# Attention scores of a hybrid decoder layer: native fp32 on 64-row tiles of TensorE in place of a two-term split

## What is computed

```python
# q: 1024 x 8 heads x 64;  k, v: 1024 x 2 kv heads x 64;  4 query heads share one kv head
scores = einsum('bnqhgd,bnkhd->bnhgqk', qb, kk) * 64 ** -0.5   # per block of 128 queries: 256 keys
scores = where((diff >= 0) & (diff < 128) & (kpos >= 0), scores, -1e30)
probs  = softmax(concat([scores, sink]))[..., :256]
out    = einsum('bnhgqk,bnkhd->bnqhgd', probs, vv)
```

## Time and profile before

| | us |
|---|---|
| median of 3 runs | 949.88 |
| lowest, highest | 949.42, 950.1 |
| the profiled execution | 949.13 |
| its span, first to last instruction | 947.3 |
| TensorE (PE) busy in it | 938.1 |
| VectorE (DVE) busy | 657.3 |
| ScalarE (ACT) busy | 435.9 |

### The profile page before, as it was taken

One profiled execution on the slowest core, in us unless ns is written; L12 is line 12 of the kernel. 1 busy time (PEld: TensorE's weight loads), 2 busy tenths in 40 slices (PEclk: granted clock), 3 DMA queues, 4 the chain that ended last, 5 costly groups with the idle time before them and its releaser, 6 DMA issues.

```text
span 947.3 us, 11501 instructions
## 1 busy us (share of the span) xinstructions
PE 938.1 (99%) x4423; PEld 778.5 (82%) x4423; DVE 657.3 (69%) x713; ACT 435.9 (46%) x651; POOL 189.3 (20%) x182
## 2 busy tenths in 40 slices
PE   8999999999999999999999999999999999999997
PEld 7988888888888888888888888888888888888886
DVE  6645797666655899777777787778776653535668
ACT  5525445544433555445444544344444454435353
POOL 3301000000111424242223243443431100000021
PEclk9999999999999999999999999999999999999999
DMA  6999971005322236386343446464647776677545
GB/s 225 271 343 213 210 145 46 23 23 178 134 89 90 89 107 205 133 190 177 123 133 100 145 118 131 107 143 111 138 90 208 212 235 210 220 267 259 186 154 200
DMA packets 114248, 151.16 MB, mean 160 GB/s; under 512 B 6289, under 2 KB 66193, under 8 KB 114193
## 3 DMA queue, kind: packets, MB, share of 16 engines
q1 hardware_dynamic: 100737, 118.63, 38.7%
q0 software_dynamic: 13456, 31.79, 16.8%
HBM read 113.17 MB, written 60.29 MB: 183 GB/s over the span
## 4 chain that ended last, share of the span: by engine, by line
PE 97%; DVE 1%; DMA 0%; ACT 0%; POOL 0%; issue 0%; DVEq 0%; POOLq 0%; SPq 0%; ACTq 0%
PE ps L1660 30%; PE ps L1661 30%; PE ps L1662 30%; PE ps L1670 1%; PE ps L1795 1%; PE ps L1818 1%; PE ps L1796 1%; PE ps L1804 1%; PE ps L1822 1%; DMA xin<-in_x 0%; DVE hlo L1168 0%; DVE ps L1185 0%; PE ps L1708 0%; DVE x2b L1471 0%; DVE x2b L1477 0%
## 5 line engine op out<-in xcount | busy, mean ns | idle before, releaser
L1660 PE MATMUL ps<-hhi,whi 128*128 128x512 f32 (+1 forms) x240 | 90.3, 376 | 0.5 <-DVE hlo L1168 0.5
L1662 PE MATMUL ps<-hhi,wlo 128*128 128x512 f32 (+1 forms) x240 | 88.5, 369 | 0.0
L1661 PE MATMUL ps<-hlo,whi 128*128 128x512 f32 (+1 forms) x240 | 88.5, 369 | 0.0
L699 POOL TENSOR_TENSOR w_sums<-wraw 128x1024 f32<-128x1024 f32 x20 | 48.4, 2421 | 185.7 <-DVE w2lo L1417 63.0
L661 POOL TENSOR_SCALAR meansq<-sumsq 128x1 f32<-128x1 f32 x28 | 9.9, 352 | 372.7 <-ACT yg L1072 170.8
L1031 ACT ACTIVATE yg<-ps,par_b 128x1024 f32<-128x1024 f32 x21 | 25.3, 1207 | 57.9 <-DVE ps L1543 57.9
L1662 PEld LDWEIGHTS ps<-hhi,wlo 128*128 128x128 f32 x240 | 45.2, 188 | 7.7
L1660 PEld LDWEIGHTS ps<-hhi,whi 128*128 128x128 f32 x240 | 45.3, 189 | 7.6 <-DVE hlo L1168 0.7
L1661 PEld LDWEIGHTS ps<-hlo,whi 128*128 128x128 f32 x240 | 45.3, 189 | 7.0
L1491 DVE SCALAR_TENSOR_TENSOR yg<-ps,par_a,yg 128x1023 f32<-128x1023 f32 x22 | 28.2, 1283 | 26.9 <-ACT yg L1031 26.9
L1660 PE MATMUL ps<-h2hi,whi 128*128 128x512 f32 x116 | 45.4, 391 | 0.2 <-DVE wraw L1178 0.2
(11 more groups left out here) (269 smaller groups left out, 2716.2 us busy)
## 6 DMA issues: line engine op xcount, KB each, us to landing
wraw<-in_ffn_w_up SPq DMA_DIRECT2D x42, 512.0 KB, 5.2
s_dram<-in_ffn_w_down POOLq DMA_DIRECT2D x6, 2816.0 KB, 27.9
wraw<-r_dram SPq DMA_DIRECT2D x44, 256.0 KB, 3.7
wraw<-s_dram SPq DMA_DIRECT2D x44, 256.0 KB, 4.8
r_dram<-cst SPq DMA_DIRECT2D x33, 256.0 KB, 2.8
wraw<-act_dram SPq DMA_DIRECT2D x33, 256.0 KB, 3.6
wraw<-in_ffn_w_down SPq DMA_DIRECT2D x33, 256.0 KB, 4.4
wraw<-in_w_in SPq DMA_DIRECT2D x14, 512.0 KB, 10.3
```

The costliest lines, as they stand in the source:

```text
L699: pool.tensor_tensor(w_sums[:, 0:2, :], raw[:, 0:4:3, :], raw[:, 2:3, :].broadcast_to([P, 2, HALF]), ALU.add)\
L1660: pe.matmul(acc, w_hi, x_hi, start=first, stop=False, skip_group_check=looped)
L1661: pe.matmul(acc, w_hi, x_lo, start=False, stop=False, skip_group_check=looped)
L1662: return pe.matmul(acc, w_lo, x_hi, start=False, stop=last, skip_group_check=looped)
```

## The change

Keys and queries are no longer split. Keys are copied as fp32 into both halves of `k_rows`; a query tile, which holds two heads, is copied as it is in one instruction into `q_rows`: head e = 0 in rows 0 to 63, head e = 1 in rows 64 to 127. A head's score is one fp32 matmul over its own 64 rows. The two heads of a pair stand next to each other in the order of issue and write to banks 4 and 5. All remainders on DVE and two semaphores go.

```diff
-        k_hi = alloc(h1, "k_hi", [P, 2, SEQ], F32R)
-        k_lo = alloc(h1, "k_lo", [P, 2, SEQ], F32R)
+        k_rows = alloc(h1, "k_rows", [P, 2, SEQ])
+        alloc(h1, "under_mix_pc", [P, 2 * SEQ])
         mix_pc = alloc(h1, "mix_pc", [P, NT, 4, P])
-        q_parts = alloc(h1, "q_parts", [P, NT, NH, P], F32R)
+        q_rows = alloc(h1, "q_rows", [P, NT, 2, 4, P])
...
-                    last = act.activation(k_hi[e * HD:(e + 1) * HD, kv, :],
+                    last = act.activation(k_rows[e * HD:(e + 1) * HD, kv, :],
                                           src[kv * HD:(kv + 1) * HD, :], ACT.Copy)
-                last.then_inc(k_rounded, 1)
+                last.then_inc(k_ready, 1)
...
-            def round_q(j):
-                src = take(use_of[2 + j])
-                for e in range(2):
-                    act.activation(q_parts[0:HD, :, 2 * j + e, :],
-                                   src[e * HD:(e + 1) * HD, :]
-                                   .rearrange("p (b c) -> p b c", b=NT), ACT.Copy)\
-                       .then_inc(q_rounded, 1)
+            def copy_q(j):
+                src = take(use_of[2 + j]).rearrange("p (b c) -> p b c", b=NT)
+                act.activation(q_rows[:, :, j // 2, j % 2, :], src, ACT.Copy).then_inc(q_ready, 1)
...
-                dve.wait_ge(k_rounded, kv + 1)
-                for e in range(2):
-                    rows = slice(e * HD, (e + 1) * HD)
-                    last = dve.tensor_tensor(k_lo[rows, kv, :], src[kv * HD:(kv + 1) * HD, :],
-                                             k_hi[rows, kv, :], ALU.subtract)
-                last.then_inc(k_ready, 1)
...
-            def low_q(j):
-                src = take(use_of[2 + j])
-                for e in range(2):
-                    dve.wait_ge(q_rounded, 2 * j + e + 1)
-                    last = dve.tensor_tensor(q_parts[HD:P, :, 2 * j + e, :],
-                                             src[e * HD:(e + 1) * HD, :]
-                                             .rearrange("p (b c) -> p b c", b=NT),
-                                             q_parts[0:HD, :, 2 * j + e, :], ALU.subtract)
-                last.then_inc(q_ready, 1)
...
-                for e in range(2):
-                    for g in range(2):
-                        at = g * 2 * P + (first - b + 1) * P
-                        acc = ps[:, 4 + e, at:(g + 1) * 2 * P]
-                        q = q_parts[:, b, 4 * kv + 2 * g + e, :]
-                        pe.matmul(acc, q, k_hi[:, kv, keys], start=True, stop=False)
-                        last = pe.matmul(acc, q, k_lo[:, kv, keys], start=False, stop=True)
+                for g in range(2):
+                    at = g * 2 * P + (first - b + 1) * P
+                    for e in range(2):
+                        rows = slice(e * HD, (e + 1) * HD)
+                        last = pe.matmul(ps[:, 4 + e, at:(g + 1) * 2 * P], q_rows[rows, b, kv, g, :],
+                                         k_rows[rows, kv, keys], start=True, stop=True)
```

More of the change, by code:

```diff
@@ L307, in build @@
         proj_done = sem("proj_done")
-        k_rounded = sem("k_rounded")
-        q_rounded = sem("q_rounded")
         k_ready = sem("k_ready")
@@ L807, in _ @@
                 for e in range(2):
-                    last = act.activation(k_hi[e * HD:(e + 1) * HD, kv, :],
+                    last = act.activation(k_rows[e * HD:(e + 1) * HD, kv, :],
                                           src[kv * HD:(kv + 1) * HD, :], ACT.Copy)
-                last.then_inc(k_rounded, 1)
+                last.then_inc(k_ready, 1)
             act.activation(v_chan, take(1), ACT.Copy).then_inc(v_ready, 1)
             round_ring(3)
-            def round_q(j):
-                src = take(use_of[2 + j])
-                for e in range(2):
-                    act.activation(q_parts[0:HD, :, 2 * j + e, :],
-                                   src[e * HD:(e + 1) * HD, :]
-                                   .rearrange("p (b c) -> p b c", b=NT), ACT.Copy)\
-                       .then_inc(q_rounded, 1)
-            round_q(0)
+            def copy_q(j):
+                src = take(use_of[2 + j]).rearrange("p (b c) -> p b c", b=NT)
+                act.activation(q_rows[:, :, j // 2, j % 2, :], src, ACT.Copy).then_inc(q_ready, 1)
+            copy_q(0)
             round_ring(4)
-            round_q(1)
+            copy_q(1)
             round_ring(5)
@@ L870, in evacuate @@
                 if s < 0:
-                    round_q(3)
+                    copy_q(3)
                 elif s < 2:
@@ L898, in _ @@
                 if u == 0:
-                    round_q(2)
+                    copy_q(2)
                 if u % 2 == 0:
@@ L1211, in _ @@
             low_ring(2)
-            src = take(0)
-            for kv in range(2):
-                dve.wait_ge(k_rounded, kv + 1)
-                for e in range(2):
-                    rows = slice(e * HD, (e + 1) * HD)
-                    last = dve.tensor_tensor(k_lo[rows, kv, :], src[kv * HD:(kv + 1) * HD, :],
-                                             k_hi[rows, kv, :], ALU.subtract)
-                last.then_inc(k_ready, 1)
             dve.wait_ge(params_in, 16 * 6)
@@ L1231, in _ @@
             low_ring(3)
-            def low_q(j):
-                src = take(use_of[2 + j])
-                for e in range(2):
-                    dve.wait_ge(q_rounded, 2 * j + e + 1)
-                    last = dve.tensor_tensor(q_parts[HD:P, :, 2 * j + e, :],
-                                             src[e * HD:(e + 1) * HD, :]
-                                             .rearrange("p (b c) -> p b c", b=NT),
-                                             q_parts[0:HD, :, 2 * j + e, :], ALU.subtract)
-                last.then_inc(q_ready, 1)
-            low_q(0)
             low_ring(4)
@@ L1246, in _ @@
                .then_inc(vt_ready, 1)
-            low_q(1)
             low_ring(5)
@@ L1388, in _ @@
                 mask_scores(u)
-                if u == 0:
-                    low_q(2)
                 if u >= 1:
@@ L1393, in _ @@
                 if u == 2:
-                    low_q(3)
                     norm_probs(u)
```

## The result

The changed kernel takes 951.85 us (median of 15 runs, 951.48 to 952.46) against 949.62 us in the same sessions: +2.2 us, ratio 1.0023, 95% interval 1.0016 to 1.0031. The forecast was +3.0 us, 952.9 us on the earlier median of 949.88. The kernel became slower, by little: the interval does not reach 1.

What follows compares the result with a forecast made beforehand. TensorE's streaming was taken to bound the kernel. Terms -1.3 (long units), -0.9 (short units), +1.8 (entries) and +3.4 (exits) gave +3.0 us, median 952.9 us, 0.3% slower; range 948.5 to 957.5.

Steps and rivals of the forecast that it cites:

- What bounds the kernel: Whole kernel: TensorE busy 938.1 of 947.3 us, so only its streaming counts; work taken from VectorE or ScalarE is worth nothing.
- Overlap of row tiles: Scores: two heads on different rows run at once, 4 x 0.216 us a unit; -1.3 us over 14 units.
- rival 1: Scores: the two heads of a pair don't run at once; +16.0 us, 965.8 us; chance 15%.
- Rival 2: Scores: heads overlap only in part, 5 steps in place of 4, by program order; +6.2 us, 956.1 us; chance 12%.
- The smaller doubt about weight loads: Scores: a step's two 128-column loads might follow one another, steps of 0.22 to 0.24 us; up to 1.3 us longer.
- The ways in and out: Around the scores: 25 new changes between full array and tiles, 9 entries and 16 exits; +5.2 us.
- Rival 3: Around the scores: mode changes cheap for row tiles; free 947.7 us, chance 6%; half-priced 950.0 us, chance 14%.
- going from `attend`'s tiles to row tiles: The 7 scores behind `attend`: entering 64-row tiles from 64-column tiles is again a change, left at 0.21 us.
- 16 exits at 0.21 = +3.4: Behind all 16 scores: return to full-width work, 14 to transposes and 2 to a projection, 0.21 us each; +3.4 us.
- 0.22 us to the second transpose: Trace sign behind a score: 0.31 us from last pair to first transpose, then 0.22 to the second.
- The row that the 0.11 was taken from: Score behind `attend`: second score matmul starts 0.23 us after the first, not 0.12; uncovered 128-column load put at 0.11.
- 0.76 on slower by more than 0.2%: Whole kernel's outcome: slower 0.76, within 0.2% 0.18, faster by over 0.2% 0.06.

Runs made afterwards that it cites:

- Experiment 1: Changed kernel plus 12 subtractions into an unread spare tile and query copies in two halves; 951.7 us, +2.1 us against the kernel before.
- Experiment 4: Changed kernel with all queries in rows 0 to 63, so all four heads use the same tile; 964.72 us, +15.1 us against the kernel before.
- experiment 2: Changed kernel with both score matmuls of the upper rows issued first, then both of the lower; 951.88 us, +2.3 us against the kernel before.
- experiment 3: Kernel before with the fp32r split kept, each head on its own 64 rows with three products; 949.74 us, +0.1 us against the kernel before.
- experiment 5: Changed kernel with each head's query padded by zeros to all 128 rows, plain fp32, no tiles; 960.72 us, +11.0 us against the kernel before.
- experiment 6: Changed kernel with the transposes moved between the two pairs of heads in 14 slots; 957.43 us, +7.7 us against the kernel before.
- experiment 7: Kernel before plus one matmul of 64 rows and 16 columns ahead of each score; 954.67 us, +4.9 us against the kernel before.

## Why the prediction was right, and where its sum was off

**What bounds the kernel** was right: nothing but TensorE's stream counts. Experiment 1 put 14 us of VectorE's work back without effect, and in the changed kernel TensorE has no wait that it had not before.

**Overlap of row tiles**, the open price, was taken from `attend`, and that held: 0.216 for a pair. Experiment 4 shows what hung on it, 12.9 us, and that rival 1 was sized rightly (15.1 against 16.0 us; most of the 0.9 is the term named below). Rival 2, overlap limited by the order of issue, is refuted by the changed kernel's own rows, four steps and not five, and by experiment 2. The smaller doubt about weight loads one after another is settled by experiment 3.

**The ways in and out**, the term that made the sign, were right in kind and in number: 16 idle times before scores, 13 of 14 seen before transposes. Experiments 5 and 6 price them at 0.16 and 0.20 us each; the first is a mean in which 14 of 25 are exits to transposes, the second has none of these. Rival 3 (cheap changes) is refuted. That going from `attend`'s tiles to row tiles costs the same as before, which was assumed, is shown by the changed kernel (113.34 to 113.88 is 0.54, as 112.36 to 112.89 was 0.53) and by experiment 7.

**The term that was mis-sized** is "16 exits at 0.21 = +3.4". Two of them precede a projection, where experiment 6 shows 0.09 + 0.11. The 14 others precede transposes. The prediction named 0.22 us to the second transpose as its sign; the trace has 0.16 where 0.11 is the distance between transposes without a change. So the uncovered load costs 0.05 to 0.06 there and not 0.11, and such an exit 0.15. 14 x 0.06 = 0.8 us less: +3.0 becomes +2.2, which is what was measured. The roundings of the other terms (0.96 for 0.95, 0.21 for 0.20) nearly cancel.

The row that the 0.11 was taken from was a way out into a score, whose load has a record of 0.19 us, and I transferred the number. A better one could have been had from the kernel before, for the loads of the transposes have records of 0.14 us there, and still have after the change:

```profile
L1804 PEld LDWEIGHTS ps<-cst,s_sb x64: 138/140/143, 85.7 to 202.1; 128*128 128x128 f32 x64
L1774 PEld LDWEIGHTS ps<-cst,s_sb x64: 137/141/143, 86.4 to 204.8; 128*128 128x128 f32 x64
```

That is the length of `attend`'s loads, 0.136, and for these the prediction had read 0.05 us uncovered. Loads with a record of 0.14 cost 0.05 where nothing covers them, loads with one of 0.19 cost 0.10 to 0.11, in all the rows shown here. This is a reading of the traces; no run changes the load of a transpose alone. The expectation of experiment 5 already uses 0.15 for this exit.

**How close it was.** The forecast had put 0.76 on slower by more than 0.2%, and that held narrowly: 0.23%, with an interval from 0.16% to 0.31%. The sign and the mechanism did not hang on that, but the choice between "slower by over 0.2%" and "within it" did come down to a few tenths of a microsecond.

## What to carry to other kernels

Array tiles are a mode, and the boundary of a stretch in that mode has a price: here 0.15 to 0.20 us for each way in or out, against 0.86 us of work inside. Count the boundaries before counting what the tiles save: here a form that streams 10% faster lost 0.26 us where it stood alone between full-width matmuls, and only 0.06 where it stood behind another tiled stretch. Take the price of a boundary from a row that has the same thing on its far side, or at least a weight load of the same length. And when one engine is busy without a wait, work that a change takes from the others is not a gain: look only at what happens to that engine's starts.

## What the runs showed of the hardware that I had not expected

- Two row tiles run fp32r matmuls at 0.12 us a pair with a load of 128 columns each (experiment 3). At full width two such loads lie 0.11 apart.
- Which matmul is a tile's partner does not hang on the order of issue over at least two matmuls (experiment 2, and `attend` in the earlier trace rows).
- 64-column tiles to 64-row tiles is as dear as tiles to full width: 0.54 us from the last four records of `attend` either way (experiment 7).
- In plain fp32 a 128x128 matmul of 256 columns costs 0.43 us whether it fills 128 rows or 64 (experiments 4 and 5, 8 steps of 0.215 and 0.216): half the rows alone save nothing.
- The uncovered load at a boundary is not one number: 0.05 us ahead of a transpose and of `attend`, 0.10 to 0.11 ahead of a score or a projection.
